# Residual stream turned token-major in a hybrid decoder layer: x and y by plain DMA, a norm per token tile, w2 and w_out products with tokens on the output partitions, and a shorter prologue

## What is computed

```python
u = modulate(rms_norm(h, g_ffn1), sh1, sc1)
h = h + 0.5 * (1 + gt1)[:, None, :] * swiglu(u, ffn1_w1, ffn1_w3, ffn1_w2)
u = modulate(rms_norm(h, g_mix), sh2, sc2)
h = h + (1 + gt2)[:, None, :] * token_mixing(u, w_in, ..., w_out)
u = modulate(rms_norm(h, g_ffn2), sh3, sc3)
h = h + 0.5 * (1 + gt3)[:, None, :] * swiglu(u, ffn2_w1, ffn2_w3, ffn2_w2)
```

## Time and profile before

| | us |
|---|---|
| median of 3 runs | 4145.31 |
| lowest and highest | 4139.47, 4584.43 |
| span of the profiled execution (slowest core) | 4141.8 |
| spans of its 8 cores | 4124.6 to 4141.8 |
| granted TensorE clock, mean of a core | 0.902 to 0.908 |

### The profile page before, as it was taken

How to read it: one execution, slowest core, us unless ns; L and a number is a source line. 1 busy time by engine, 2 the same in 40 slices (tenths; PEclk the granted TensorE clock), 3 DMA queues, 4 the chain that set the end, 5 groups by cost and what they waited for, 6 DMA issues and landing times.

```text
span 4141.8 us, 57046 instructions; the slowest of 8 cores (4124.6 to 4141.8 us)
## 1 busy us (share of the span) xinstructions
PE 3538.7 (85%) x18152; PEld 1700.0 (41%) x18152; DVE 1597.7 (39%) x2837; ACT 1424.3 (34%) x2510; POOL 380.2 (9%) x232
## 2 busy tenths in 40 slices
PE   2599996887787979999947999878877787999998
PEld 1244442553333433444433444335433333434444
DVE  1522225557444444222243222355654444432223
ACT  1410105653666343101033101165546654331011
POOL 0022121000000000111001111100000000011110
PEclk9899998876788989999978999977778889999999
DMA  5334342001110433222134222200001022522223
GB/s 152 117 122 143 112 143 72 28 22 36 31 41 17 159 112 110 77 85 75 40 122 133 60 92 67 87 32 12 22 31 62 13 87 87 180 82 62 81 67 107
DMA packets 370385, 329.35 MB, mean 80 GB/s; under 512 B 23808, under 2 KB 361728, under 8 KB 370096
## 3 DMA queue, kind: packets, MB, share of 16 engines
q1 hardware_dynamic: 370096, 325.70, 25.3%
HBM read 308.90 MB, written 16.78 MB: 79 GB/s over the span
## 4 chain that ended last, share of the span: by engine, by line
PE 71%; ACT 11%; DVE 7%; issue 6%; DMA 3%; SPq 1%; DVEq 0%; ACTq 0%
PE ps L129 71%; ACT u L129 3%; ACT t_2 L129 2%; ACT t_3 L129 2%; DVE arena L129 2%; DVE t_0 L129 1%; DVE t_1 L129 1%; DMA stg<-w_mod 1%; ACT t_0 L129 1%; ACT L129 1%; SPq L129 1%; DVE Sst L129 1%; DMA wb<-x 1%; ACT wb L129 1%; ACT t_1 L129 1%
## 5 line engine op out<-in xcount | busy, mean ns | idle before, releaser
L129 PE MATMUL ps<-u,wb 128*128 128x512 bf16 x9024 | 2086.8, 391 | 90.9 <-ACT wb L129 43.3
L129 PEld LDWEIGHTS ps<-u,wb 128*128 128x128 bf16 x9024 | 895.8, 100 | 1205.6 <-issue 220.1
L129 PE MATMUL ps<-arena,wb 128*128 128x512 bf16 x3968 | 881.9, 379 | 0.0
L129 POOL CAST wb<-stg 128x2048 bf16<-128x2048 f32 (+3 forms) x228 | 380.0, 1676 | 3701.7 <-PE ps L129 2663.5
L129 PEld LDWEIGHTS ps<-arena,wb 128*128 128x128 bf16 x3968 | 387.4, 98 | 466.1 <-issue 2.1
L129 ACT ACTIVATE t_0<-ps 128x512 f32<-128x512 f32 (+1 forms) x272 | 162.3, 597 | 769.1 <-PE ps L129 636.6
L129 DVE SCALAR_TENSOR_TENSOR h<-ps,Gmod,h 128x512 f32<-128x512 f32 x320 | 240.2, 751 | 476.4 <-PE ps L129 476.0
L129 DVE TENSOR_TENSOR arena<-ps,t_0 128x512 bf16<-128x512 f32 x152 | 105.0, 691 | 299.3 <-PE ps L129 235.2
L129 DVE TENSOR_TENSOR arena<-ps,t_1 128x512 bf16<-128x512 f32 x152 | 104.6, 688 | 266.2 <-PE ps L129 234.2
L129 ACT ACTIVATE t_1<-ps 128x512 bf16<-128x512 f32 (+1 forms) x144 | 85.9, 597 | 284.8 <-PE ps L129 284.0
L129 PE MATMUL ps<-t_0,ones_bf 128*64 128x128 bf16 (+1 forms) x204 | 66.1, 367 | 111.3 <-DVE t_0 L129 81.1
(11 more groups left out here) (134 smaller groups left out, 3135.6 us busy)
## 6 DMA issues: line engine op xcount, KB each, us to landing
stg<-ffn_w SPq DMA_DIRECT2D x88, 1024.0 KB, 5.5
stg<-w_in SPq DMA_DIRECT2D x66, 1024.0 KB, 5.2
stg<-w_mod SPq DMA_DIRECT2D x36, 1024.0 KB, 6.3
stg<-ffn_w SPq DMA_DIRECT2D x32, 768.0 KB, 5.2
stg<-ffn_w SPq DMA_DIRECT2D x32, 640.0 KB, 4.6
stg<-w_branch_gla SPq DMA_DIRECT2D x16, 1024.0 KB, 7.6
stg<-w_out SPq DMA_DIRECT2D x16, 1024.0 KB, 5.3
wb<-x SPq DMA_DIRECT2D x22, 512.0 KB, 7.6
```

The source lines that it names most:

```text
L129: r = getattr(eng, it["fn"][0])(**it["fn"][1])
```

## The change

- `h` becomes token-major, 16 tiles of 128 tokens with 1024 columns. `load_x` and `store_y` are one DMA each, straight to and from `h`, with no transpose and no copy.
- The norm works on one token tile (`norm_tile`). `prep` on it: ScalarE Square with an accumulated row sum, Ln and Exp on that one column, VectorE multiply of the tile by it into bf16. `turn`, called some units later (`defer`, `tick`): eight bf16 transposes into four PSUM banks that stay held for a group of four tiles, and after the fourth tile eight evictions, four on ScalarE and four on VectorE, that apply scale and shift and write `u`. `u` stays feature-major.
- w2 and w_out products have tokens on the output partitions: `gbuf` or `merged` is stationary, the weights are the moving operand. The gate now varies along columns, so it is multiplied into the weights by GpSimd instead: `make_Gb` spreads `Gmod` to a row on all partitions (`gsh`) with VectorE and eight f32 products, once per residual update and sequence.
- The FFN runs in three parts of 8, 8 and 6 blocks, and w2 has a buffer of its own. The next norm's tiles are placed in the last part's w2 products (before attention, and before the next sequence) or in the second column half of w_out.
- At the end of the second FFN each finished token tile is stored at once, its x of the next sequence is loaded three tiles later and normed six tiles later.
- All weight tiles go through one prefetch order (`get`, `rel`, `pump`), cast by GpSimd, in the merge too.
- Prologue: the small vectors come as rows into one tile and are turned by one transpose; 8 tiles of w_mod are loaded at once into the idle arena and `stg`. Tiles 8 to 11 follow in the first FFN (`run_bg(5)`), with the gate row behind them.

The core of the diff (functions that only moved, or whose names of buffers changed, are left out):

```diff
-        def load_x(b, tts=range(16), between=None):
-                for half in range(2):
-                    pb, pk, _ = bank()
-                    for j in range(4):
-                        dc = half * 4 + j
-                        pg.op("pe", ("transpose", dict(
-                            out=pb[:, j * P:(j + 1) * P], in_=xs[:, dc * P:(dc + 1) * P], identity=ident)),
-                            [skey, "cst"], [pk])
...
+            def load_x(b, tt):
+                pg.dma(("dma_start", dict(out=h[:, tt, :], in_=x[b, tt * P:(tt + 1) * P, :])), f"h{tt}",
+                       writes=[("h", tt, 0), ("h", tt, 1)])
+
+            def store_y(b, tt):
+                pg.dma(("dma_start", dict(out=y[b, tt * P:(tt + 1) * P, :], in_=h[:, tt, :])), f"h{tt}",
+                       reads=[("h", tt, 0), ("h", tt, 1)])
...
+            def prep(l, tt):
+                xn, xk = xbuf(l, tt % 4)
+                hk = [("h", tt, 0), ("h", tt, 1)]
+                pg.op("act", ("activation", dict(out=xn, in_=h[:, tt, :], func=AF.Square,
+                                                 accum_out=ssq[:, tt:tt + 1])), hk, [xk, ("ssq", tt)])
+                pg.op("act", ("activation", dict(out=rr[:, tt:tt + 1], in_=ssq[:, tt:tt + 1], func=AF.Ln,
+                                                 bias=kst[:, 0:1], scale=1.0 / D)), [("ssq", tt), "kst0"], [("rr", tt)])
+                pg.op("act", ("activation", dict(out=rr[:, tt:tt + 1], in_=rr[:, tt:tt + 1], func=AF.Exp, scale=-0.5)),
+                      [("rr", tt)], [("rr", tt)])
+                pg.op("dve", ("tensor_scalar", dict(out=xn, in0=h[:, tt, :], scalar1=rr[:, tt:tt + 1], scalar2=None,
+                                                    op0=ALU.mult)), hk + [("rr", tt)], [xk])
...
+                for dc in range(DC):
+                    bi = bks[dc // 2][2]
+                    o0 = bi * 2 * TS + (dc % 2) * TS + k * P
+                    pg.op("pe", ("transpose", dict(out=psum16[:, o0:o0 + P], in_=xn[:, dc * P:(dc + 1) * P],
+                                                   identity=ident_bf[:])), [xk, "identbf"], [bks[dc // 2][1]])
+                if k < 3:
+                    return
...
+                    if (dc // 2) % 2 == 0:
+                        pg.op("act", ("activation", dict(out=u[:, dc, sl], in_=src, func=AF.Identity, bias=B_, scale=A_)),
+                              rd, [("u", g)])
+                    else:
+                        pg.op("dve", ("tensor_scalar", dict(out=u[:, dc, sl], in0=src, scalar1=A_, scalar2=B_,
+                                                            op0=ALU.mult, op1=ALU.add)), rd, [("u", g)])
...
+                    for tt in range(16):
+                        ts = tt // 4
+                        for dh in range(2):
+                            po, pok, _ = bank()
+                            for fl in range(nf):
+                                mm(po, gbuf[:, fl, tt * P:(tt + 1) * P], w2buf[:, fl, dh * 512:(dh + 1) * 512],
+                                   fl == 0, fl == nf - 1, [("g", fl, ts), ("w2", fl // 2)], [pok])
+                            pg.op("dve", ("tensor_tensor", dict(
+                                out=h[:, tt, dh * 512:(dh + 1) * 512], in0=po, in1=h[:, tt, dh * 512:(dh + 1) * 512],
+                                op=ALU.add)), [pok, ("h", tt, dh)], [("h", tt, dh)])
+                        if last:
+                            tail(tt)
+                        tick()
...
+                def tail(tt, b=b):
+                    store_y(b, tt)
+                    if b + 1 < nbr:
+                        defer(3, lambda: load_x(b + 1, tt))
+                        defer(6, lambda: norm_tile(0, b + 1, tt, 2))
```

More of the change, by code:

```diff
@@ L362, in mod_fin @@
-        def mod_fin(l):
-            coef = 1.0 if l == 1 else 0.5
-            for b in range(NB):
-                pg.op("dve", ("scalar_tensor_tensor", dict(
-                    out=Amod[:, l, :, b], in0=modT[:, l * 24 + 8:l * 24 + 16, b], scalar=1.0, in1=gT[:, l, :],
-                    op0=ALU.add, op1=ALU.mult)), [("modT", l, b), ("gT", l)], [("Amod", l, b)])
-                pg.op("dve", ("tensor_scalar", dict(
-                    out=Gmod[:, l, :, b], in0=modT[:, l * 24 + 16:l * 24 + 24, b], scalar1=1.0, scalar2=coef,
-                    op0=ALU.add, op1=ALU.mult)), [("modT", l, b)], [("Gmod", l, b)])
@@ L497, in build_nc @@
[L497 removed]
         KB = 512
+        gbuf = arena[:, 0:32 * KB].rearrange("p (f t) -> p f t", f=8)
+        w2buf = arena[:, 32 * KB:48 * KB].rearrange("p (f d) -> p f d", f=8)
         acc = arena[:, 0:32 * KB].bitcast(F32).rearrange("p (c o t) -> p c o t", c=2, o=2)
@@ L509, in build_nc @@
         merged = arena[:, 40 * KB:56 * KB].rearrange("p (c t) -> p c t", c=8)
+        FFN_KEYS = [("g", f, t) for f in range(8) for t in range(NTS)] + [("w2", i) for i in range(4)]
+        PST_KEYS = [("pst", i) for i in range(7)]
         ACC_KEYS = [("acc", ch, t) for ch in range(2) for t in range(NTS)]
@@ L914, in merge_out @@
-                for dp in range(4):
-                    tasks.append(([(kc_view(w_out, dp * 256, 256), DC, 256, "act")],
-                                  lambda ws, dp=dp: comp_o(ws, dp)))
-                run_tasks(tasks)
-                if after_half is not None:
-                    after_half(th)
-        def dump(slot_i, b):
-            if dbg and b == 0:
-                pg.dma(("dma_start", dict(out=dbg_out[slot_i].rearrange("p (c t) -> p c t", c=DC), in_=h[:])), "dbg",
-                       reads=[("h", t) for t in range(NTS)])
@@ new lines, in merge_out @@
+                            pg.op("dve", ("tensor_tensor", dict(
+                                out=h[:, tt, dh * 512:(dh + 1) * 512], in0=po, in1=h[:, tt, dh * 512:(dh + 1) * 512],
+                                op=ALU.add)), [pok, ("h", tt, dh)], [("h", tt, dh)])
+                            if dh == 1:
+                                norm_tile(2, b, tt, 2)
+                            tick()
+                        rel(wos[0][1], wos[1][1])
+            prologue_mod()
+            if order:
+                pump(2)
@@ new lines, in generate @@
+            for tt in range(4, 8):
+                load_x(0, tt)
+            if order:
+                pump(4)
+            for tt in range(8, 16):
+                load_x(0, tt)
+            for tt in range(8):
+                norm_tile(0, 0, tt, 99)
+            ensure_u(1)
+            for tt in range(8, 16):
+                defer(tt // 4, lambda tt=tt: norm_tile(0, 0, tt, 99))
+            for b in range(nbr):
+                ffn(0, 0, b, lambda tt: norm_tile(1, b, tt, 2))
+                run_bg(len(bg))
+                pg.transfer(FFN_KEYS, MIX_A)
```

1323 lines of the change are left out of this document (710 added, 613 removed).

## The result

The changed kernel is faster: its time is 0.9661 of the kernel before, 95% interval 0.9595 to 0.9728. The lowest run is 3983.22 us, and the profiled execution spans 3981.6 us against 4141.8. (Executions in which the cores of a die ran at a lower clock are left out of the ratio; they are why the median of all five, 4124.47, says little.) The forecast was 3910, with a range of 3838 to 3985: the sign was right, but the span fell by 160.2 us where I had worked out 234.5. So 74.3 us are to be found.

What follows compares the result with a forecast made beforehand. TensorE, 71% of the chain, bounds the kernel, so time is won only outside its full stream: 537.5 us of losses become 303, 234.5 off 4141.8 gives 3907, with 3.5 around the span 3910 us; range 3838 to 3985.

Steps and rivals of the forecast that it cites:

- The 537.5 us of losses: Time outside TensorE's full stream before: prologue 180.3, norms before attention 105, after merge halves 95, sequence change 130.7, end 26.5.
- The loop's mechanism: Norm loop before attention: VectorE's multiply waits for ScalarE's chain, holding back the next evictions; 4.65 us a tile, 72 in all.
- The prices of GpSimd's multiply and of Square: Prices used: GpSimd's weight multiply by a gate row 4.3 us, ScalarE's 1024-column Square 1.05 us.
- x came in time: Sequence change: a rival claimed x reloads come late behind stores, a tile taking 5.2 us, +32, 3942; chance 0.10.
- the slower rival: At w_out: GpSimd's multiply outlasts its cover; gain gone at 21.6 us each, 4280 us at 30; chance 0.02.
- The meetings of VectorE with GpSimd: Norm loop: a tensor_scalar meeting a GpSimd cast costs 1 us more; some 20 meetings, 20 us, only in the range.
- a quarter of the four u evictions (0.6 to 0.69): Norm loops: each tile's share of a group's evictions into u, one addend of the 4.65 us a tile before attention.
- The gate row (make_Gb) before FFN2: Two rounds of VectorE multiply, four f32 products, VectorE copy before FFN2; some 5 us, twice 10.
- The two before the merge: Gate rows before the merge: set equal to the wait for ScalarE's first cast, which they replace.
- The prologue: Start of the kernel: first product at 66 us, later a stall of 18.5 and a gate row 5; sum 105.
- The upper end of the range: 3985: 34 for tensor_scalar at the slow rate, 13 for the accumulator, half the clock's 98 less what overlaps.
- The clock rival: Norm loops: the clock falls to 1.2 GHz because TensorE idles a third of each tile; up to 4008; chance 0.12.

Runs made afterwards that it cites:

- e2: Changed kernel with VectorE's multiply of a token tile, and its transposes, placed one tile later (not at the change of sequence); 3942.5 us, 35.3 less.
- e1: Changed kernel with a key of its own for each of the eight evictions that write u for a group; 3929.6 us, 48.2 less.
- e9: Changed kernel with gate rows' VectorE multiplies first, products and copies later (not in the prologue), scratch in small temporaries; 3933.5 us, 44.3 less.
- e6: Gate rows' multiplies first, products and copies later (prologue's not delayed), on the changed kernel with e1, e2 and e3 together; 3818.2 us, 55.2 less than that.
- e10: Changed kernel with the edits of e1 and e9 together; 3879.4 us, 98.4 less, 0.9383 of the kernel before.
- e8: Changed kernel with the norm before attention placed behind the last w2 products instead of between them; 3978.8 us against 3977.8.
- e3: Changed kernel with gate-row scratch in small temporaries where free, and the first weight pair given back sooner in the first FFN part; 3973.5 us, 4.3 less.
- e12: Changed kernel with two keys for u, one for ScalarE's evictions and one for VectorE's; 3938.9 us, 38.9 less.

## Why the prediction was right and wrong

Right:
- What goes. The 537.5 us of losses went, and the rest of the program kept its 3604 us, in the sum.
- The loop's mechanism: "VectorE's order is eviction, eviction, then the tensor_scalar of that same tile". An ordinary tile by the rows is 1.28 + 0.15 + 1.93 + 0.75 = 4.11; without the share for `u` my sum was 3.97. The accumulator's own operation, which I took at nothing, is 0.19 of it. e2 won 35 us by taking this wait out, nearly all of it behind the merges.
- The prices of GpSimd's multiply and of Square; x came in time (9.3 us to land against 7.6 in the earlier trace rows, but between the group ends the tiles at the change of sequence run 3.04 us apart, TensorE's pace), and the slower rival had no ground.
- The meetings of VectorE with GpSimd, 20 us in the range, came to little: the multiply into the temporaries averages 0.83 us over 64 where the one into `arena` takes 0.75, 5 us in all. The 0.69 named there as the undisturbed time is a row of another operation; the squares into `t_1` average 0.68, so the reading holds.

Wrong, by the size of each:
- "a quarter of the four u evictions (0.6 to 0.69)". This step failed. I took the eight evictions of a group as two queues side by side, a share of 0.65 us a tile. They are one chain of 6 us, on which PSUM banks hang, so TensorE stops at each fourth tile. In the sum nothing stood for that stop: there are 24 groups, and e1 shows 48 us net, won at the places at which the table above is over. The diff showed it: both engines' evictions write `[("u", g)]`.
- "The gate row (make_Gb) before FFN2 adds ... some 5 us". This term was too small. e9 shows for the six rows 44 us beyond their own products. I had 5 for each of four. By stage e9 wins 7 in the prologue and 20 at the three others of them; with some 2 of products each they cost 35 in place of 20. The two before the merge I had set equal to the wait that they replace. That did not hold: they cost 13 us more, which the rest of the span hides as a balance, and e9 wins 19 there.
- The prologue: its stall is 29.8 us for 23.5 (18.5 and 5). The reason given was right (loads behind loads), but the row waited for the staging buffer too. And the first product starts at 72.1 where I had 66.
- The upper end of the range: its terms, 34 + 13 + 49, are 96, and it was set 75 above the forecast with "less what overlaps", for which no number stood.
- The clock rival was set apart as a case of its own (0.12). It is not a case but an addition to each stall: the mean granted clock is 0.77 at 1410 to 1425 us, where a group's evictions stop TensorE, and e6 won twice the idle time that it removed. At the first of these places:

```profile
1414.39 0.27 PE L129 MATMUL ps<-ident_bf,t 128*128 128x128 bf16 x2 [2.06 <-ACT u L129]
...
1418.91 3.62 PE L129 MATMUL ps<-wb,arena 128*128 128x512 bf16 x8
```

The Trainium skill describes a clock that goes down and up with short idles between groups of products ("TensorE: Matmul & The Clock Gate", "A second HAM failure mode: psum-queue depth-cycling"). The trace agrees: after four stops of 0.9 to 2.1 us for PSUM banks, eight products take 3.62 us, the price of 1.2 GHz.

Chain 48 and rows 15 are 63 of the 74.3; the rest is the prologue and terms of a few us with both signs, which no run separates. e10 bears out the size and not the sum to a us: it won 94 us by the slowest core and ends 19 below the forecast, since its edits also remove what I had priced rightly and the rows before the merges.

## What to carry to other kernels

Where several engines write parts of one tile, look at the key or semaphore that each write takes before you count them as parallel: a shared key turns queues into a chain, and what it holds (here PSUM banks) decides who stops. Price a short TensorE pause by its length and by the products that follow it at half clock; here that doubled it. Look where in the program a small difference lies before you call it a gain: an untouched stretch moved by 5 us with the clock. And work moved between products earns only what its own waits leave: undo the move by itself (e8) before you build on it.

## What the hardware showed that was not expected

- Square with an accumulated row sum is followed by an operation of its own, ACTIVATION_READ_ACCUMULATOR, 0.19 us, and a 1-column Ln takes 0.29 against 0.20 for the Exp.
- Granted clocks are not only 1.00 and 0.50. In e3, on core 1 and in the same way on core 0, TensorE was busy without a gap and had 0.81 for over 100 us; cores 2 to 7 had no such stretch, and core 2 had 1.00 there. In e9 to e12 it shows as well, on neighbouring pairs of cores, for stretches of 4 to 15 us. A product took 0.26 us for 0.216. Windows of e3, core 1, then core 2:

```profile
180.00:284.00 104.00, 104.00 (x485) 44.49 (x484) 26.37 (x49) 6.57 (x11) 33.26 (x14) 0.81 0.44 135
300.00:350.00 50.00, 50.00 (x251) 22.85 (x249) 9.81 (x16) 8.76 (x15) 15.57 (x6) 1.00 0.35 106
```

```profile
200.00:280.00 80.00, 79.51 (x449) 37.37 (x455) 27.08 (x50) 4.16 (x7) 27.50 (x11) 1.00 0.44 140
```

What sets it, no run shows. In e3 the slowest core, one of the two, is 16 us slower than the median, which is why medians of cores are compared here.
- In e8 the norm's transposes, with nothing else on TensorE, stay at half clock, 1.01 us for eight. TensorE also waits between them, being busy 5.05 of 14 us, so this does not tell whether transposes count for the clock, the question of the prediction; no run here has transposes alone without waits between them. Window of e8, core 2:

```profile
594.00:608.00 14.00, 5.05 (x40) 3.89 (x41) 6.62 (x10) 11.49 (x26) 0.00 (x0) 0.50 0.00 0
```
